# Hybrid decoder layer: the fourth weight sum of the down projection made by accumulating transfers instead of VectorE additions

## The chip, the cores and the metric

The kernel runs on one core of a Trainium2 chip. The metric is the device time of one execution in microseconds, the median of several runs.

## The reference, cut to what matters

One decoder layer in float32: a mixer (short gated convolution beside an mLSTM), a layer norm, a gated MLP with a causal convolution of width 3, and a second layer norm. The change touches only the MLP's last product.

```python
D_MODEL, SEQ, D_FF = 2048, 512, 5632

def conv_ffn(x, w_up, w_ffn_conv, b_ffn_conv, w_down):
    hid = jnp.einsum('bsd,df->bsf', x, w_up)
    hid = causal_dwconv(hid, w_ffn_conv, b_ffn_conv)
    val, gate = hid[..., :D_FF], hid[..., D_FF:]
    return jnp.einsum('bsf,fd->bsd', jax.nn.silu(gate) * val, w_down)

x = layer_norm(alpha * x + mix, ln1_g, ln1_b)
ff = conv_ffn(x, w_up, w_ffn_conv, b_ffn_conv, w_down)
x = layer_norm(alpha * x + ff, ln2_g, ln2_b)
```

## The kernel before

The down projection multiplies the hidden activations (512 tokens by 5632 features) with `w_down` (5632 by 2048). It is a block scheme with seven products in place of eight. The weights are cut into four blocks, A11, A12, A21 and A22, and the products run in the order P1, P2, P6, P5, P7, P3, P4. Products need sums of weight blocks:

- S1: `da21 += w_down[A22]`, an accumulating transfer that GpSimd issues (`down_s1`, L691).
- S2: `dx = da21 + da11`, a VectorE addition (`down_s2`, L1679). P6 reads `dx`.
- S3: `da11 += w_down[A21]`, an accumulating transfer (`down_s3`, L699). P7 reads it.
- S4: `da12 += dx`, a VectorE addition (`down_s4`, L1685). P3 reads it.

The features go through in six chunks of 4, 4, 4, 4, 3 and 3 pairs of 128-row tiles. A slot is one pair of one product: a [128, 1024] weight tile and twelve matmuls of 512 columns. With the products numbered k = 7 * chunk + place, product k of a four-pair chunk has four slots. For each slot ScalarE copies the weight tile to `dslot_hi` in float32r (`down_split`, L1084), VectorE makes the remainder `dslot_lo` (`down_lo_part`, L1655), and TensorE multiplies hi by hi, hi by lo and lo by hi (L1781 to L1783). Both splits run four slots ahead. For each product the hidden block is split likewise (`hid_split` L1101, `hid_lo_part` L1663 and L1666), one product ahead. VectorE adds product k from PSUM to `acc` in the loop of product k + 1 (`add_out`, L1698; ScalarE copies the four first touches, L1127). Product k on TensorE waits until the additions of product k - 2 are done, because PSUM has two sets of banks.

The sums of hidden blocks (T1 to T4, L706, L712, L719, L725) are GpSimd additions of [128, 1024]; in chunk 0 VectorE makes T1 and T2. The residual is added to `acc` by four accumulating transfers of 1 MB (`add_residual`, L732), issued by GpSimd in chunks 0 and 1.

The order of every engine is written out by hand. On GpSimd a chunk is: T1, T2, S3 for pairs 0 and 1, S3 for the rest, T3, T4, then the two S1 of the next chunk, with the residual transfers in between. On SP the loads of the next chunk follow in the order `hb11` (waits for T4), `da21`, `hb12`, `da11`, `hb22`, `da12`, `hb21`, `da22`; the `hb` loads wait for a hidden split and the `da` loads for a slot's `down_lo`. On VectorE the additions S2 and S4 stand after the last slot of a product:

```python
if i in (1, 2, 3) and p == g - 1:
    todo += [("S4", c, a) for a in {1: [0], 2: [1, 2], 3: [3]}[i] if a < g]
if i in (5, 6) and p == g - 1 and c + 1 < CHUNKS:
    todo += [("S2", c + 1, a) for a in {5: [0, 1], 6: [2]}[i]]
```

Accumulating transfers go from GpSimd's queue (q0, software_dynamic), SP's loads from q1 (hardware_dynamic), and both use the same 16 DMA engines.

Of the kernel before, what the change touches and what calls it, by code (L numbers as in the profile page):

```python
# [7 lines left out]
ALU = mybir.AluOpType  # L8
# [26 lines left out]
CHUNK_PAIRS = [4, 4, 4, 4, 3, 3]  # L35
# [95 lines left out]
def build(nc, x_t, x_rows, w_mix, w_out, w_up, w_down, b_gates, conv_w, gain, ln1_cols, ffn_conv,  # L131
          ln1_rows, ln2_rows, ident_in, head_rows_in, causal_in, out):
    ctx = ExitStack()
    with ctx:
# [3 lines left out]
        def sem(name):  # L138
            return ctx.enter_context(nc.semaphore(name))
# [75 lines left out]
        da12 = at("da12", [P, 4, 1024], XB + 16 * KB)  # L215
        da21 = at("da21", [P, 4, 1024], XB)
        da22 = at("da22", [P, 4, 1024], XB + 32 * KB)
        dx = at("dx", [P, 4, 1024], XB + 48 * KB)
# [33 lines left out]
        tile_hi, tile_lo, tile_done = sem("tile_hi"), sem("tile_lo"), sem("tile_done")  # L252
        pads = sem("pads")
        gate_lo, gate_dve, gate_act = sem("gate_lo"), sem("gate_dve"), sem("gate_act")
        gates_ready, gate_turned, gate_cols_ready = sem("gates_ready"), sem("gate_turned"), sem("gate_cols_ready")
        vp_hi, vp_lo, o_sig = sem("vp_hi"), sem("vp_lo"), sem("o_sig")
        qk_h, qk_l = sem("qk_h"), sem("qk_l")
        g_spread, decay_arg, decay_exp, decay_ready = sem("g_spread"), sem("decay_arg"), sem("decay_exp"), sem("decay_ready")
# [31 lines left out]
        acc_in = [sem(f"acc_in{i}") for i in range(4)]  # L290
        s1_added = [sem(f"s1_added{i}") for i in range(2)]
        s3_added = [sem(f"s3_added{i}") for i in range(2)]
        s2_down, s4_down = sem("s2_down"), sem("s4_down")
        t1_sum, t2_sum, t3_sum, t4_sum = sem("t1_sum"), sem("t2_sum"), sem("t3_sum"), sem("t4_sum")
        hc_lo = sem("hc_lo")
        down_hi, down_lo, down_done, half_done = sem("down_hi"), sem("down_lo"), sem("down_done"), sem("half_done")
# [52 lines left out]
        def slot_no(c, i, p):  # L349
            return SLOT0[c] + i * CHUNK_PAIRS[c] + p  # L350
# [10 lines left out]
        def sums_after(s):  # L361

            c, i, p = DOWN[s]
            g = CHUNK_PAIRS[c]
            todo = []
            if i == 0 and c == 0:
                todo.append(("S2", 0, p))
            elif i == 0 and p == 3:
                todo.append(("S2", c, 3))
            if i in (1, 2, 3) and p == g - 1:  # L370
                todo += [("S4", c, a) for a in {1: [0], 2: [1, 2], 3: [3]}[i] if a < g]
            if i in (5, 6) and p == g - 1 and c + 1 < CHUNKS:
                todo += [("S2", c + 1, a) for a in {5: [0, 1], 6: [2]}[i]]
            return todo
# [222 lines left out]
        def _(pool):  # L597
# [96 lines left out]
            def down_s3(c, p):  # L694
# [4 lines left out]
                pool.dma_start(da11[:, p:p + w, :], w_down[A21, :, 1024 * n:1024 * (n + w)].rearrange("p (k n) -> p k n", k=w),  # L699
                               accum_op=ALU.add, max_dma_last_dim=4096).then_inc(s3_added[p // 2], 16)  # L700

            def down_t1(c, g):
                for b in range(2):
                    pool.wait_ge(hb_in[b], 16 * (c + 1))
                pool.wait_ge(hc_lo, NP * c)
                pool.tensor_tensor(hy[:, 0:g, :], hb12[:, 0:g, :], hb11[:, 0:g, :], ALU.subtract).then_inc(t1_sum, 1)  # L706
# [7 lines left out]
            def down_t3(c, g):  # L714
                pool.wait_ge(hb_in[3], 16 * (c + 1))
                pool.wait_ge(t1_sum, OUT_CHUNKS + c + 1)
                if c == 0:
                    pool.wait_ge(down_lo, slot_no(0, 3, 0))
                pool.tensor_tensor(hb12[:, 0:g, :], hb22[:, 0:g, :], hb12[:, 0:g, :], ALU.subtract).then_inc(t3_sum, 1)  # L719
# [16 lines left out]
            for c in range(CHUNKS):  # L736
                g = CHUNK_PAIRS[c]
                if c:
                    down_t1(c, g)
                    down_t2(c, g)  # L740
                for p in range(0, g, 2):
                    down_s3(c, p)
                down_t3(c, g)
                if c == 1:
                    add_residual(0, 1, NP)
                down_t4(c, g)
                if c == 0:
                    add_residual(0, 0, 2)
                if c + 1 < CHUNKS:
                    for p in range(0, CHUNK_PAIRS[c + 1], 2):  # L750
                        down_s1(c + 1, p)
                if c == 0:
                    add_residual(1, 1, 5)
                    add_residual(1, 0, 6)
# [10 lines left out]
        def _(act):  # L765
# [299 lines left out]
            def down_split(s):  # L1065

                c, i, p = DOWN[s]
                what = ORDER[i]
                if s < DOWN_SLOTS:
                    act.wait_ge(up_done, min(N_UP - 2 + s, N_UP))  # L1070
                else:
                    act.wait_ge(down_done, s - DOWN_SLOTS + 1)
                n = sum(CHUNK_PAIRS[:c]) + p
                if what in ("P1", "P2", "P4"):
                    if p == 0:
                        act.wait_ge(da_in[BLOCK[what]], 16 * (c + 1))
                elif what in ("P5", "P7"):
                    if p % 2 == 0:
                        act.wait_ge({"P5": s1_added, "P7": s3_added}[what][p // 2],
                                    16 * (OUT_CHUNKS + sum(CHUNK_PAIRS[a] > p for a in range(c + 1))))  # L1080
                else:
                    act.wait_ge({"P6": s2_down, "P3": s4_down}[what], n + 1)
                src = (da11, da12, da21, da22, dx)[BLOCK[what]]
                act.activation(dslot_hi[s % DOWN_SLOTS][:, :], src[:, p, :], ACT.Copy).then_inc(down_hi, 1)  # L1084

# [59 lines left out]
        def _(dve):  # L1145
# [96 lines left out]
            def mix_work(n):  # L1242
                kind = MIX[n]
                if n - 1 in LAST_QK:
                    h = LAST_QK[n - 1]
                    dve.wait_ge(decay_ready, h + 1)
                    for j in range(NS):
                        dve.wait_ge(scores_done, NS * h + j + 1)
                        s = sc[:, SC_AT[j]:SC_AT[j] + SC_W[j]]
                        dve.scalar_tensor_tensor(s, ps[:, B_S + j % 2, 0:SC_W[j]], Q_SCALE, s, ALU.mult,  # L1250
                                                 ALU.mult).then_inc(p_raw, 1)
                if n == GATES:
                    gates_a()
                if kind[0] == "v" and kind[2] == 3:
                    for c in range(NS):
                        dve.wait_ge(vp_hi, NS * kind[1] + c + 1)
                        dve.tensor_tensor(v_lo[:, c, :, 0:HD], ps[:, B_V + c, :].rearrange("p (h e) -> p h e", h=2),
                                          v_hi[:, c, :, 0:HD].bitcast(F32), ALU.subtract).then_inc(vp_lo, 1)
                if n == GATES + 4:
                    dve.wait_ge(gate_turned, 1)  # L1260
                    dve.tensor_copy(gate_cols[:, :, :, :], ps[:, B_TURN, 0:32].rearrange("p (a c h) -> p a c h", a=2, c=NS)
                                    ).then_inc(gate_cols_ready, 1)
                    dve.wait_ge(gate_cols_ready, 1)
                if kind[0] == "qk":
                    dve.wait_ge(qk_h, 4 * kind[1] + kind[2] + 1)
                    dve.tensor_tensor(qk_lo[:, kind[2], :], ps[:, B_V + kind[2], :],
                                      qk_hi[:, kind[2], :].bitcast(F32), ALU.subtract).then_inc(qk_l, 1)
                h = LAST_QK.get(n)
                if h is not None:
                    dve.wait_ge(g_spread, h + 1)  # L1270
                    if h:
                        dve.wait_ge(p_h, h)
                    for j in range(NS):

                        last = dve.tensor_scalar(sc[:, SC_AT[j]:SC_AT[j] + SC_W[j]], ps[:, B_S, P * j:SEQ],
                                                 gate_cols[:, 0, j, h:h + 1], 0.0, ALU.subtract, ALU.max)
                    last.then_inc(decay_arg, 1)
# [391 lines left out]
            def down_s2(c, p):  # L1669

                if p == 0:
                    dve.wait_ge(da_in[A11], 16 * (c + 1))
                if p % 2 == 0:
                    dve.wait_ge(s1_added[p // 2], 16 * (OUT_CHUNKS + sum(CHUNK_PAIRS[a] > p for a in range(c + 1))))
                if c:
                    dve.wait_ge(s4_down, sum(CHUNK_PAIRS[:c]))
                else:
                    dve.wait_ge(up_done, N_UP - NP + 4)
                dve.tensor_tensor(dx[:, p, :], da21[:, p, :], da11[:, p, :], ALU.add).then_inc(s2_down, 1)  # L1679

            def down_s4(c, p):
                n = sum(CHUNK_PAIRS[:c]) + p
                dve.wait_ge(s2_down, n + 1)
                dve.wait_ge(down_lo, slot_no(c, 1, p) + 1)
                dve.tensor_tensor(da12[:, p, :], da12[:, p, :], dx[:, p, :], ALU.add).then_inc(s4_down, 1)  # L1685

            def add_out(k, u):

# [47 lines left out]
            for s in range(N_DOWN):  # L1736
# [17 lines left out]
                if s == 1:  # L1754
# [1 line left out]
                    dve.wait_ge(t1_sum, OUT_CHUNKS + 1)  # L1756
                    dve.wait_ge(hc_lo, 1)
                    dve.tensor_tensor(hb11[:, 0:g, :], hb22[:, 0:g, :], hy[:, 0:g, :], ALU.subtract).then_inc(t2_sum, 1)
                for what, chunk, pair in sums_after(s):
                    (down_s2 if what == "S2" else down_s4)(chunk, pair)  # L1760
            out_var(0, 12)
            out_var(1, 12)
            finish(0)
# [437 lines left out]
```

## Time and profile before

| what | value |
|---|---|
| median of 3 runs | 2173.48 us (2172.08 to 2177.03) |
| span of the profiled execution | 2176.2 us |
| down projection and last norm in it | from about 1725 us to the end |
| TensorE busy | 2125.9 us, 98% |
| VectorE busy | 1594.2 us, 73% |
| GpSimd busy | 267.1 us, 12% |
| S4 additions on VectorE | 22, 1211 ns each |

The profiled execution has its span alone; it is 2.7 us over the median of the runs and within their spread. Times of the trace are microseconds from the span's start. In a timeline row the two numbers are start and duration, and the bracket at the end is the idle time of the engine ahead of the instruction and what ended it. DMA share is the mean busy share of the 16 DMA engines; over 1.0 means that they were busy without a break.

### The profile page before, as it was taken

What the parts mean: (1) busy time and instruction counts of PE and PEld (TensorE: products, weight loads), DVE (VectorE), ACT (ScalarE), POOL (GpSimd) and SP (SyncE); (2) the same over time, 40 slices, a digit from 0 to 9 for tenths busy, and PEclk for the clock granted to TensorE, in tenths of its full rate; (3) what the DMA queues carried; (4) which work ended last, traced back from release to release, by engine and by line L of the source; (5) the groups of instructions that cost most, each with busy time, mean ns of one, the idle gap of its engine ahead of it and who ended that gap; (6) DMA issues with size and microseconds to landing.
All of it is one profiled execution on the core that took longest, in us unless ns stands there. A gap on an engine that the chain in (4) does not pass through costs nothing. (4 is left out here: it accounts for less than half of the span.)

```text
span 2176.2 us, 26843 instructions
## 1 busy us (share of the span) xinstructions
PE 2125.9 (98%) x10583; PEld 1789.3 (82%) x10583; DVE 1594.2 (73%) x1860; ACT 948.3 (44%) x1107; POOL 267.1 (12%) x241
## 2 busy tenths in 40 slices
PE   9999999999999998999999999999999999999995
PEld 7888888888888887788888888888888788888874
DVE  4354324423338997988888888888888789999998
ACT  3332222221124446555555555555555464444442
POOL 0000000000001304011111111111111023221220
PEclk9999999999999999999999999999999999999998
DMA  6222222242227626888888887887778888775463
GB/s 238 97 97 78 92 89 91 78 171 98 98 79 232 181 73 162 219 241 231 218 207 210 238 219 197 212 229 209 187 203 209 274 228 219 210 237 145 140 193 78
DMA packets 93754, 375.88 MB, mean 173 GB/s; under 512 B 8908, under 2 KB 21228, under 8 KB 80320
## 3 DMA queue, kind: packets, MB, share of 16 engines
q1 hardware_dynamic: 63328, 263.22, 34.4%
q0 software_dynamic: 30304, 110.99, 26.3%
q8 instruction: 82, 1.34, 0.3%
q14 instruction: 40, 0.33, 0.0%
HBM read 326.46 MB, written 26.21 MB: 162 GB/s over the span
## 5 line engine op out<-in xcount | busy, mean ns | idle before, releaser
L1787 PE MATMUL ps<-xb,slot_hi 128*128 128x512 f32 x2408 | 854.5, 400 | 10.2 <-DVE hid L1532 9.8
L1788 PE MATMUL ps<-xb,slot_lo 128*128 128x256 f32 x2400 | 674.4, 281 | 0.0
L1787 PEld LDWEIGHTS ps<-xb,slot_hi 128*128 128x128 f32 x2408 | 453.8, 188 | 126.3 <-issue 12.5
L1788 PEld LDWEIGHTS ps<-xb,slot_lo 128*128 128x128 f32 x2400 | 454.1, 189 | 0.0
L772 ACT ACTIVATE w_hi<-raw 128x2048 fp32r<-128x2048 f32 x56 | 107.3, 1917 | 424.5 <-PE ps L1783 422.0
L1154 DVE TENSOR_TENSOR w_lo<-raw,w_hi 128x2048 fp32r<-128x2048 f32 x55 | 125.8, 2287 | 213.7 <-ACT w_hi L772 213.7
L1781 PE MATMUL ps<-act_hi,w_hi 128*128 128x512 f32 x640 | 249.7, 390 | 0.0
L1783 PE MATMUL ps<-act_hi,w_lo 128*128 128x512 f32 x640 | 249.1, 389 | 0.0
L1782 PE MATMUL ps<-act_lo,w_hi 128*128 128x512 f32 x640 | 249.1, 389 | 0.0
L1501 DVE TENSOR_TENSOR slot_lo<-unit_odd,slot_hi 128x1024 fp32r<-128x1024 f32 x153 | 187.0, 1222 | 36.6 <-ACT slot_hi L974 36.4
L974 ACT ACTIVATE slot_hi<-unit_odd 128x1024 fp32r<-128x1024 f32 x154 | 162.7, 1057 | 106.6 <-PE ps L1788 79.0
L1501 DVE TENSOR_TENSOR slot_lo<-unit_even,slot_hi 128x1024 fp32r<-128x1024 f32 x147 | 179.6, 1222 | 36.0 <-ACT slot_hi L974 35.9
L974 ACT ACTIVATE slot_hi<-unit_even 128x1024 fp32r<-128x1024 f32 x147 | 155.3, 1057 | 93.8 <-PE ps L1788 79.2
L1532 DVE TENSOR_TENSOR hid<-hid,ps 128x256 f32<-128x256 f32 x301 | 126.0, 419 | 42.8 <-ACT hid L1008 32.1
L1781 PE MATMUL ps<-slot_hi,hc 128*128 128x512 f32 x372 | 145.6, 391 | 5.3 <-DVE acc L1698 4.1
L1008 ACT ACTIVATE hid<-ps 128x256 f32<-128x256 f32 x172 | 65.7, 382 | 188.3 <-PE ps L1788 188.3
L1782 PE MATMUL ps<-slot_lo,hc 128*128 128x512 f32 x372 | 144.8, 389 | 0.0
L1783 PE MATMUL ps<-slot_hi,hc 128*128 128x512 f32 x372 | 144.8, 389 | 0.0
L1781 PEld LDWEIGHTS ps<-act_hi,w_hi 128*128 128x128 f32 x640 | 120.1, 188 | 27.0 <-issue 2.3
L1783 PEld LDWEIGHTS ps<-act_hi,w_lo 128*128 128x128 f32 x640 | 120.1, 188 | 24.9
L1782 PEld LDWEIGHTS ps<-act_lo,w_hi 128*128 128x128 f32 x640 | 120.2, 188 | 24.6
L1542 DVE SCALAR_TENSOR_TENSOR yy<-hid,fc,yy 128x511 f32<-128x511 f32 (+1 forms) x172 | 128.4, 747 | 3.9 <-ACT yy L1020 0.9
(238 smaller groups left out, 3431.8 us busy)
## 6 DMA issues: line engine op xcount, KB each, us to landing
raw<-w_mix SPq DMA_DIRECT2D x56, 1024.0 KB, 4.9
unit_odd<-w_up SPq DMA_DIRECT2D x88, 512.0 KB, 6.4
unit_even<-w_up SPq DMA_DIRECT2D x84, 512.0 KB, 6.5
da<-w_down SPq DMA_DIRECT2D x16, 2048.0 KB, 12.6
unit_odd<-w_up POOLq DMA_DIRECT2D x44, 512.0 KB, 8.8
unit_even<-w_up POOLq DMA_DIRECT2D x42, 512.0 KB, 8.4
da<-w_down POOLq DMA_DIRECT2D x20, 1024.0 KB, 9.8
oa<-w_out SPq DMA_DIRECT2D x6, 2048.0 KB, 8.1
```

Source lines behind the costliest of these rows:

```text
L772: act.activation(w_hi[:, s % SPLIT, :], raw[:, s % RAW, :], ACT.Copy).then_inc(tile_hi, 1)
L974: act.activation(slot_hi[(n + 2) % 3][:, :], unit[m % 2][:, BLOCK[ORDER[i]], :], ACT.Copy).then_inc(up_hi, 1)
L1008: act.activation(hid[g % 2][:, t, 256 * half:256 * half + 256], ps[:, up_bank(m, i), 0:256], ACT.Copy).then_inc(hid_act, 1)
L1154: dve.tensor_tensor(w_lo[:, s % SPLIT, :], raw[:, s % RAW, :], w_hi[:, s % SPLIT, :].bitcast(F32), ALU.subtract).then_inc(tile_lo, 1)
L1501: dve.tensor_tensor(lo_slot(n)[:, :], unit[m % 2][:, BLOCK[ORDER[i]], :], slot_hi[(n + 2) % 3][:, :].bitcast(F32), ALU.subtract).then_inc( ...
L1532: dve.tensor_tensor(x, x, cross, ALU.add).then_inc(hid_dve, 1)
L1542: dve.scalar_tensor_tensor(yy[:, t, lag:SEQ], hid[g % 2][:, t, 0:SEQ - lag], fc[:, c + 2 - lag:c + 3 - lag], yy[:, t, lag:SEQ], ALU.mult, ...
L1781: pe.matmul(dst, a[0], b[0], start=first, stop=False, skip_group_check=onto)
L1782: pe.matmul(dst, a[0], b[1], start=False, stop=False, skip_group_check=onto)
L1783: return pe.matmul(dst, a[1], b[0], start=False, stop=last, skip_group_check=onto)
L1787: pe.matmul(dst, a[0], b, start=first, stop=False, skip_group_check=onto)
L1788: return pe.matmul(dst[:, 256:512], a[1], b[:, 0:256], start=False, stop=last, skip_group_check=onto)
```

## The change

The 22 VectorE additions of S4 are taken out. Twelve accumulating transfers take their place, two a chunk, each adding one or two pairs of `dx` to `da12`, from SBUF to SBUF. GpSimd issues them behind T3 and ahead of T4 (in chunk 1 ahead of the residual transfer that stands there too). The semaphore `s4_down` becomes two, one for each half. P3's split on ScalarE and the next chunk's S2 on VectorE wait for the transfer's landing. A semaphore of the gates in the mixer (`gate_cols_ready`) is merged into `gate_dve`, which makes room for the new one.

```diff
-            if i in (1, 2, 3) and p == g - 1:
-                todo += [("S4", c, a) for a in {1: [0], 2: [1, 2], 3: [3]}[i] if a < g]
...
+            def down_s4(c, p):
+
+                n, w = sum(CHUNK_PAIRS[:c]) + p, min(2, CHUNK_PAIRS[c] - p)
+                pool.wait_ge(s2_down, n + w)
+                pool.wait_ge(down_lo, slot_no(c, 1, p) + w)
+                pool.dma_start(da12[:, p:p + w, :], dx[:, p:p + w, :], accum_op=ALU.add, max_dma_last_dim=4096
+                               ).then_inc(s4_down[p // 2], 16)
...
                 down_t3(c, g)
+                for p in range(0, g, 2):
+                    down_s4(c, p)
                 if c == 1:
                     add_residual(0, 1, NP)
                 down_t4(c, g)
...
-                else:
-                    act.wait_ge({"P6": s2_down, "P3": s4_down}[what], n + 1)
+                elif what == "P6":
+                    act.wait_ge(s2_down, n + 1)
+                elif p % 2 == 0:
+                    act.wait_ge(s4_down[p // 2], 16 * sum(CHUNK_PAIRS[a] > p for a in range(c + 1)))
...
-                                    ).then_inc(gate_cols_ready, 1)
-                    dve.wait_ge(gate_cols_ready, 1)
+                                    ).then_inc(gate_dve, 1)
+                    dve.wait_ge(gate_dve, 29)
...
                 if c:
-                    dve.wait_ge(s4_down, sum(CHUNK_PAIRS[:c]))
+                    dve.wait_ge(s4_down[p // 2], 16 * sum(CHUNK_PAIRS[a] > p - p % 2 for a in range(c)))
...
-            def down_s4(c, p):
-                n = sum(CHUNK_PAIRS[:c]) + p
-                dve.wait_ge(s2_down, n + 1)
-                dve.wait_ge(down_lo, slot_no(c, 1, p) + 1)
-                dve.tensor_tensor(da12[:, p, :], da12[:, p, :], dx[:, p, :], ALU.add).then_inc(s4_down, 1)
```

## Rows read from the trace of the kernel before

**Rows 1.** The page: busy time, share of the span and instructions.

```profile
PE 2125.9 (98%) x10583; PEld 1789.3 (82%) x10583; DVE 1594.2 (73%) x1860; ACT 948.3 (44%) x1107; POOL 267.1 (12%) x241
```

**Rows 2.** Windows: stretch, its length, busy time by engine, PEclk, DMA share, GB/s.

```profile
1900.00:1975.00 75.00, 75.00 (x333) 62.10 (x332) 70.65 (x57) 36.40 (x35) 16.91 (x8) 1.00 0.65 193
...
2100.00:2150.00 50.00, 46.96 (x205) 38.35 (x206) 47.54 (x49) 19.82 (x20) 2.75 (x1) 1.00 0.02 5
```

**Rows 3.** Timeline of TensorE: four matmuls that had waited for VectorE.

```profile
1760.59 0.47 PE L1781 MATMUL ps<-slot_hi,hc 128*128 128x512 f32 x1 [0.21 <-DVE acc L1698]
...
1826.58 0.47 PE L1781 MATMUL ps<-slot_hi,hc 128*128 128x512 f32 x1 [0.47 <-DVE acc L1698]
...
2101.34 0.47 PE L1781 MATMUL ps<-slot_hi,hc 128*128 128x512 f32 x1 [1.38 <-DVE acc L1698]
...
2127.87 0.47 PE L1781 MATMUL ps<-slot_hi,hc 128*128 128x512 f32 x1 [1.70 <-DVE acc L1698]
```

**Rows 4.** The tile `dx`: durations min/median/max in ns, first and last start.

```profile
L1679 DVE TENSOR_TENSOR dx<-da,da x22: 1209/1217/3404, 1737.7 to 2092.4; 128x1024 f32<-128x1024 f32 x22
L1685 DVE TENSOR_TENSOR da<-da,dx x22: 1208/1211/1219, 1752.5 to 2121.1; 128x1024 f32<-128x1024 f32 x22
```

**Rows 5.** Timeline of VectorE, last chunk.

```profile
2110.72 0.96 DVE L1663 SCALAR_TENSOR_TENSOR hc<-hy,hc 128x768 fp32r<-128x768 f32 x1 [0.20 <-ACT hc L1101]
...
2119.97 2.35 DVE L1685 TENSOR_TENSOR da<-da,dx 128x1024 f32<-128x1024 f32 x2
...
2126.51 1.21 DVE L1698 TENSOR_TENSOR acc<-acc,ps 128x1024 f32<-128x1024 f32 x1
```

**Rows 6.** Timeline of GpSimd: T3, T4, the S1 transfers, T3 of the last chunk.

```profile
1752.74 5.49 POOL L719 TENSOR_TENSOR hb<-hb,hb 128x1024 f32<-128x1024 f32 x1 [4.38 <-DVE slot_lo L1655]
1758.18 3.39 POOL L725 TENSOR_TENSOR hy<-hb,hb 128x1024 f32<-128x1024 f32 x1
...
1777.99 2.42 POOL L691 DMA_DIRECT2D da<-w_down  x2 [15.27 <-DMA da<-w_down]
...
2094.54 2.17 POOL L719 TENSOR_TENSOR hb<-hb,hb 128x768 f32<-128x768 f32 x1
2111.86 2.75 POOL L725 TENSOR_TENSOR hy<-hb,hb 128x768 f32<-128x768 f32 x1 [15.15 <-DVE hc L1663]
```

**Rows 7.** DMA queues, 1892 to 1904, then 1624 to 1632 us: packets, MB, share.

```profile
q0 software_dynamic: 272, 1.05, 49.7%
...
q0 software_dynamic: 322, 1.12, 72.7%
```

**Rows 8.** Windows by DMA load, columns as in rows 2.

```profile
1760.00:1764.00 4.00, 3.79 (x17) 2.89 (x16) 4.00 (x4) 3.33 (x4) 2.71 (x2) 1.00 0.27 82
1764.00:1828.00 64.00, 63.53 (x281) 52.32 (x280) 55.80 (x43) 34.57 (x35) 16.38 (x10) 1.00 1.03 280
1832.00:1850.00 18.00, 18.00 (x81) 14.92 (x80) 18.00 (x16) 8.63 (x9) 4.82 (x3) 1.00 0.58 188
...
1904.00:1910.00 6.00, 6.00 (x28) 4.99 (x27) 6.00 (x6) 3.23 (x4) 2.85 (x1) 1.00 0.00 0
```

**Rows 9.** DMA queues, 1784 to 1796 us.

```profile
q0 software_dynamic: 374, 1.46, 60.8%
q1 hardware_dynamic: 372, 2.06, 43.8%
```

**Rows 10.** Timeline of VectorE where chunk 0 passes into chunk 1.

```profile
1793.03 2.35 DVE L1679 TENSOR_TENSOR dx<-da,da 128x1024 f32<-128x1024 f32 x2
...
1799.84 1.21 DVE L1698 TENSOR_TENSOR acc<-acc,ps 128x1024 f32<-128x1024 f32 x1
...
1819.07 3.97 DVE L1655 TENSOR_TENSOR slot_lo<-dx,slot_hi 128x1024 fp32r<-128x1024 f32 x1
```

**Rows 11.** Timeline of ScalarE there: two hidden splits.

```profile
1793.56 1.06 ACT L1101 ACTIVATE hc<-hb 128x1024 fp32r<-128x1024 f32 x1 [1.71 <-PE ps L1783]
...
1808.76 1.06 ACT L1101 ACTIVATE hc<-hb 128x1024 fp32r<-128x1024 f32 x1 [6.02 <-DMA hb<-h_dram]
```

More of the change, by code:

```diff
@@ L254, in build @@
         gate_lo, gate_dve, gate_act = sem("gate_lo"), sem("gate_dve"), sem("gate_act")
-        gates_ready, gate_turned, gate_cols_ready = sem("gates_ready"), sem("gate_turned"), sem("gate_cols_ready")
+        gates_ready, gate_turned = sem("gates_ready"), sem("gate_turned")
         vp_hi, vp_lo, o_sig = sem("vp_hi"), sem("vp_lo"), sem("o_sig")
@@ L292, in build @@
         s3_added = [sem(f"s3_added{i}") for i in range(2)]
-        s2_down, s4_down = sem("s2_down"), sem("s4_down")
+        s2_down, s4_down = sem("s2_down"), [sem(f"s4_down{i}") for i in range(2)]
         t1_sum, t2_sum, t3_sum, t4_sum = sem("t1_sum"), sem("t2_sum"), sem("t3_sum"), sem("t4_sum")
@@ L1758, in _ @@
                     dve.tensor_tensor(hb11[:, 0:g, :], hb22[:, 0:g, :], hy[:, 0:g, :], ALU.subtract).then_inc(t2_sum, 1)
-                for what, chunk, pair in sums_after(s):
-                    (down_s2 if what == "S2" else down_s4)(chunk, pair)
+                for _, chunk, pair in sums_after(s):
+                    down_s2(chunk, pair)
             out_var(0, 12)
```

## The prediction

> **What bounds the kernel now.** I read the page first. TensorE is busy for 98% of the span [rows 1]. So an edit counts only where TensorE waits, or where it makes TensorE wait. The windows of the down projection say how much is left to win: in chunks 2 and 3 TensorE has 75.00 busy us in 75.00, its clock granted in full, though VectorE works 70.65 of them [rows 2]. VectorE is nearly full there and still costs nothing. The loss sits at the edges. The timeline of TensorE has waits for the additions to `acc` of 0.21, 0.47, 1.38 and 1.70 us [rows 3] and one more of 0.24, together 4.0. That is all that a relieved VectorE could give in the steady part; the tail behind the last product has no S4 in it.
>
> **What is removed.** 22 additions of 1.21 us [rows 4], which overlap by some 0.08, so about 25 us of VectorE time. Only those are worth anything that stand between VectorE's last idle moment and a wait of TensorE.
> - Last chunk, product P7: VectorE was idle for 0.20 until 2110.72, and from there it runs without a break to the addition at 2126.51, for which TensorE waits 1.70. The pair of S4 at 2119.97 stands in that run [rows 5]. The next instruction starts at 2122.24, so their place is worth 2.27, more than the wait: minus 1.70.
> - Chunk 0, the wait at 1760.59: one S4 at 1752.5 [rows 4] is ahead of it: minus 0.21.
> - The waits at 1826.58 and 2101.34: VectorE has idle moments (at 1812 and 1814, at 2067 and 2075) between the last S4 and them. They stay.
> - The other S4 are hidden under a TensorE that is busy throughout [rows 2]: nothing.
>
> Sum of the removal: minus 1.9 us. If I am wrong on the waits that stay, at most minus 4.0.
>
> **What is added on GpSimd.** Twelve issues, some 1.2 us each by the pair of S1 issues (2.42 for two [rows 6]). Behind them stands T4. In the last chunk GpSimd is idle 15.15 us ahead of T4, and in the chunks from 1 on the idle time there is 8 to 15 us: nothing. In chunk 0 T4 starts straight after T3 [rows 6]; it moves by 2.4 us, from 1758.2 to 1760.6, with the residual transfer and SP's `hb11` load behind it. `hb11` is next needed by T1 at 1802: nothing by itself. A DMA issue does not stretch VectorE's instructions in the trace, while a GpSimd addition does: the remainder at 1819.07 takes 3.97 instead of 1.21 [rows 10]. S4 is a transfer, so nothing is added of that.
>
> **What is added on the DMA engines.** This is the price. No S4 of this size is in the trace; the nearest row is one S3, 1.05 MB accumulated by itself: 49.7% of 12 us, so 6.0 us of all 16 engines [rows 7]. The source there is HBM and for S4 it is SBUF; the half-size sums from SBUF in the up projection ran among others at a similar rate (1.12 MB at 72.7% of 8 us, which is 5.5 us for 1.05 MB [rows 7]). I take 6.0; bounds 5 and 7. A four-pair chunk adds 12 us of DMA work, a three-pair chunk 9.
> - Chunks 2 to 5: S4 follows T3, as at 1896.8, and the engines are idle soon after (share 0.00 from 1904 to 1910 [rows 8]). The transfer lands within some 15 us of T3's end, P3 is split 28 us after it. In the last chunk T3 ends at 2096.7 [rows 6], the window behind has a share of 0.02 [rows 2], and P3's split comes near 2126. Hidden.
> - Chunk 0: T3 ends at 1758.2 [rows 6], the first packets go near 1760. Until 1764 the engines have a share of 0.27, and from 1764 to 1828 it is 1.03, with no idle time in 64 us [rows 8]. Of 12 us some 3 fit ahead; 9 go into a full queue. That is the stretch in which chunk 1 is loaded.
> - Chunk 1: its S4 go out near 1822, with 12 us more; in 1832 to 1850 a share of 0.58 leaves 7.6 us [rows 8], so some 4 us stay when chunk 2 is loaded.
>
> **Who is late.** S1 of chunk 1 was issued at 1777.99 [rows 6], when its load had landed and GpSimd's queue was empty. Now S4 and the residual stand ahead of it in that queue. The two queues take turns: 374 packets against 372 in 12 us, and the software queue's share is 60.8% [rows 9]. The 9 us left shrink by some 2 for the moment in which the queue had stood empty: 7 of work, which is 7 us if the loads lose their place and 11 if they keep half. I take 8. By packet counts the first S1 had landed near 1791 to 1793, and S2 reads it on VectorE at 1793.03 [rows 10] with next to no room. So S2 begins 6 to 8 us late, say 7. Queued behind it on VectorE are the hidden remainder of product 7 and the additions of product 5, which end at 1801.1 [rows 10]; they end at 1808.1. TensorE starts products every 10.88 us; it left one at 1793.3, just ahead of the ScalarE split that it released [rows 11], and wants product 7 at 1804.2. That is a wait of 3.9.
>
> Late next is `hb21`, for which ScalarE waited 6.02 us until 1808.76 [rows 11]. TensorE needs it, split, for product 8 near 1815, or 1819 after the first wait: 3 us are needed for the splits, so the landing may slip by 7. It slips by 7 to 9: 0 to 2, say 0.7. Last, VectorE has 15 us of work from there to the additions of product 7, stretched by T3 (3.97 for one remainder [rows 10]), against 13 that TensorE leaves it: a wait of 2 at product 9 where 0.47 stood, plus 1.5. At the passage to chunk 2, S2 starts at 1869.9 and the later of its two blocks had landed at 1864.0: 6 us of room for the 4 that are left, so nothing.
>
> Sum: minus 1.9, plus 3.9, plus 0.7, plus 1.5, is plus 4.2. On the profile's span 2176.2 gives 2180.4; on the median of the runs, 2.7 lower, it is 2177.7, which I round to 2177.5.
>
> In the Trainium skill ("DMA: Bandwidth & Descriptors", section "Anatomy of one DMA") a transfer on GpSimd's queue is fitted as 2.0 us plus its bytes by 436 GB/s; by that S4 would move in 2.4 us and the two would nearly fit the idle moment, so the time would fall by the 1.9 alone. The trace disagrees: the lone S3 took 6.0 us of the engines. The same page's section "Queues, rings and completion order" says that each engine serves its queues in turns, packet by packet; by that rule, which the equal packet counts here bear out, the loads do not shield S1 from what stands ahead of it.
>
> **The rivals.**
> - *The queue absorbs it* (28 in 100). For it: S1 may have landed earlier than the packet counts say, TensorE has 3 us of room at product 7, and the sum from SBUF may be cheaper. From a delay of S1 of under 4 us TensorE sees nothing. Then minus 1.9 stands alone, with 0 to 1 lost at product 9: 2171.5 to 2173. Against it: a share of 1.03 for 64 us [rows 8]. The page's fit would put the time here.
> - *The backlog runs on into chunk 2* (13 in 100). If the hidden loads of 1 KB packets each wait for a 4 KB accumulate, `hb21` slips by 12 or more, and S4 of chunk 1 does the same to chunk 2. Then 5 more at product 8 and 2 to 4 at chunk 2: 2183 to 2187.
> - *The other side: faster by over 0.2%* (3 in 100). VectorE's relief would have to remove all five waits, 4.0, and GpSimd's T3 in the last chunk would have to meet VectorE more kindly. It decides when TensorE waits no longer at 2101, where two S2 and a remainder stretched by T3 [rows 6] make the lateness without any S4: about 2169.
> - *S4 lands late for P3 of chunk 0.* ScalarE wants its second half at 1777.2 and it lands near 1772 to 1778. A late one eats four slots of lead (10.9 us) first: nothing. It is part of the forecast.
>
> **The numbers.** My forecast, 2173 to 2182, has 56 in 100. The 80% range takes in the absorbed case and the start of the heavy one: 2171.0 to 2184.0. A measurement of this kernel can tell about 0.2%, 4.3 us, so slower begins at 2177.8, in the middle of the forecast. Slower: half of the forecast less a little (27) and all of the heavy case (13), 40. Same: the rest of the forecast (29) and the absorbed case (28), 57. Faster: 3.
>
> **What would show it.** Right: no L1685 on VectorE and its busy time some 25 us lower; L1679 near 1793 idle before it for 5 us or more until a transfer lands; a TensorE wait of 3 to 4 us near 1804 and a longer one near 1829; the software queue busy without a gap from 1760 to about 1850; the wait of 1.70 at P7 of the last chunk gone and the 1.38 ahead of it still there; chunks 2 and 3 unchanged, TensorE full. Wrong: S2 of chunk 1 on time with S4 in the queue (then the sum from SBUF is cheaper than 6 us or the queues don't share as I think), or a ScalarE wait for S4 ahead of P3.

## The result and the profile after

The changed kernel is slower: ratio 1.0047 to the kernel before, 95% interval 1.0031 to 1.0062 (medians of twelve runs each 2187.15 and 2172.78 us). On the 2173.5 of the prediction the ratio gives 2183.7, 0.3 us inside its range; the median itself lies above it. The sign is that of the forecast. The size is 10 us by the ratio (14 by the medians), where 4 were forecast.

The page of the profile after, busy time as in [rows 1]:

```profile
PE 2128.0 (97%) x10583; PEld 1791.9 (82%) x10583; DVE 1572.7 (72%) x1838; ACT 949.7 (43%) x1107; POOL 277.3 (13%) x253
```

VectorE is 21.5 us less busy, with 22 instructions fewer. The span is 9.3 us longer. In this execution the down projection also began 1.3 us earlier than in that of before, so times of the two traces are compared with that in mind. The waits of TensorE in the down projection, timeline rows that answer to [rows 3]:

```profile
1824.58 0.76 PE L1785 MATMUL ps<-slot_hi,hc 128*128 128x512 f32 x1 [10.67 <-ACT acc L1137]
...
1825.57 0.63 PE L1787 MATMUL ps<-slot_hi,hc 128*128 128x512 f32 x1
...
2112.58 0.47 PE L1785 MATMUL ps<-slot_hi,hc 128*128 128x512 f32 x1 [1.38 <-DVE acc L1702]
```

One wait of 10.67 us is new: it is the start of product 8, P2 of chunk 1. The 0.21, the 0.47 and the 1.70 of before are gone; the 1.38 has stayed, and so have two small ones, 0.24 ahead of it and one at 2042 in the trace before (0.31) and at 2053 after (0.46). The windows say two more things (columns as in [rows 2]):

```profile
1764.00:1824.00 60.00, 49.91 (x220) 40.84 (x218) 38.25 (x30) 24.07 (x25) 11.60 (x7) 0.96 1.05 287
...
1824.00:1828.00 4.00, 3.42 (x8) 2.78 (x9) 3.37 (x4) 4.00 (x5) 0.00 (x0) 0.50 0.37 138
...
1900.00:1975.00 75.00, 75.00 (x333) 62.10 (x332) 66.37 (x53) 36.38 (x35) 19.28 (x10) 1.00 0.81 224
```

The loss sits in 1764 to 1824, where the DMA engines have no idle moment (share 1.05). Chunks 2 and 3 run with TensorE full, as before. And behind its wait TensorE gets half its clock (0.50, the level of 1.2 GHz): its matmuls start 0.43 us apart instead of 0.23 until 1829.4, some 11 of them at about 0.2 more each, which costs 2.3 us.

The chain that ended last, in the same stretch, names what TensorE waited for (start, duration, what):

```profile
1783.60 35.96 DMA hb<-h_dram
...
1820.62 1.04 ACT slot_hi L1094
1821.66 0.91 ACT acc L1137
...
1823.42 1.02 ACT acc L1137
...
1824.58 0.76 PE ps L1785
```

The load of `hb21` took 36.0 us from its issue; it was 23.6 before. ScalarE stood at the hidden split that reads it, the second row here answering to [rows 11]; ahead of it is the last slot split before the wait:

```profile
1800.24 1.07 ACT L1094 ACTIVATE slot_hi<-da 128x1024 fp32r<-128x1024 f32 x1 [1.65 <-PE ps L1787]
1819.66 1.06 ACT L1111 ACTIVATE hc<-hb 128x1024 fp32r<-128x1024 f32 x1 [18.36 <-DMA hb<-h_dram]
```

Behind that split in ScalarE's order stand a slot split, a first-touch copy of product 6, another slot split and the second copy. TensorE's product 8 waits for both copies, because they empty the PSUM banks that it writes. So its wait is put down to a ScalarE copy, while the cause is a transfer four instructions ahead of it.

GpSimd, in answer to [rows 6]:

```profile
1756.05 2.42 POOL L705 DMA_DIRECT2D da<-dx  x2
1757.56 3.36 POOL L731 TENSOR_TENSOR hy<-hb,hb 128x1024 f32<-128x1024 f32 x1
1759.90 2.18 POOL L738 DMA_DIRECT2D acc<-res_dram  x1
...
1782.29 2.42 POOL L689 DMA_DIRECT2D da<-w_down  x2 [20.21 <-DMA da<-w_down]
```

And the DMA queues, in windows of 1764 to 1776, 1776 to 1784 and 1808 to 1816 us (columns as in [rows 7]):

```profile
q0 software_dynamic: 511, 1.99, 89.9%
q1 hardware_dynamic: 474, 0.53, 15.3%
...
q1 hardware_dynamic: 774, 3.40, 103.5%
q0 software_dynamic: 9, 0.00, 0.3%
...
q0 software_dynamic: 378, 1.42, 88.9%
q1 hardware_dynamic: 379, 0.39, 17.4%
```

The first pair shows the mechanism. S4 and the residual transfer keep GpSimd's queue full while SP's queue holds `hb11`, in 512 packets of 1 KB. While both have work, the two queues move nearly equal numbers of packets, so that 0.53 MB of loads move beside 1.99 MB of sums; before, the same 12 us moved 2.52 MB of loads beside 1.04 MB. The second pair shows GpSimd's queue empty: S1 can only be issued when `da21` has landed, at 1782.3 instead of 1778.0, and it found nothing ahead of it. The third pair is `hb21` itself: 379 packets of 1 KB against 378 that are nearly all of 4 KB.

VectorE at the passage, in answer to [rows 10]:

```profile
1794.60 2.36 DVE L1689 TENSOR_TENSOR dx<-da,da 128x1024 f32<-128x1024 f32 x2 [2.92 <-DMA da<-w_down]
...
1801.42 1.21 DVE L1702 TENSOR_TENSOR acc<-acc,ps 128x1024 f32<-128x1024 f32 x1
```

S2 waited 2.92 us for S1. By the clock it began only 1.6 us later than before; against TensorE, which ran 1.4 us earlier here, it was 3.0 late. TensorE did not feel it.

### The profile page after: what moved, and what is told of

It is laid out like the page before. It is cut to its first block and busy times, and to the rows that moved or that the text cites. A ratio compares the mean times of both kernels' runs of the same rounds, so it can differ in the third digit from the quotient of the medians.

```text
span 2185.5 us, 26813 instructions
## 1 busy us (share of the span) xinstructions
PE 2128.0 (97%) x10583; PEld 1791.9 (82%) x10583; DVE 1572.7 (72%) x1838; ACT 949.7 (43%) x1107; POOL 277.3 (13%) x253
## 5 line engine op out<-in xcount | busy, mean ns | idle before, releaser
L1511 DVE TENSOR_TENSOR slot_lo<-unit_even,slot_hi 128x1024 fp32r<-128x1024 f32 x147 | 179.7, 1223 | 35.6 <-ACT slot_hi L982 35.4
L1785 PE MATMUL ps<-slot_hi,hc 128*128 128x512 f32 x372 | 146.5, 394 | 13.7 <-ACT acc L1137 10.7
## 6 DMA issues: line engine op xcount, KB each, us to landing
da<-w_down SPq DMA_DIRECT2D x16, 2048.0 KB, 12.9
```

Source lines behind the costliest of these rows:

```text
L1511: dve.tensor_tensor(lo_slot(n)[:, :], unit[m % 2][:, BLOCK[ORDER[i]], :], slot_hi[(n + 2) % 3][:, :].bitcast(F32), ALU.subtract).then_inc( ...
L1785: pe.matmul(dst, a[0], b[0], start=first, stop=False, skip_group_check=onto)
```

## The experiments

Runs of one kernel spread over up to 19 us here, and in several kernels they lie in two groups about 8 us apart (the twelve of e11: six from 2163.7 to 2168.0, six from 2173.1 to 2176.6). The profiles place this spread mostly ahead of the down projection, which began between 1715 and 1728 us. So beside each ratio stands the length of the down projection in the profiled run, from the first to the last start of a matmul that reads `hc`. It was 427.4 us before and 437.9 after. Each kernel has one profiled execution; the ratios rest on twelve runs of each kernel, nine of e2 and four of e9.

| kernel | ratio | 95% interval | down projection, us | wait at product 8, us |
|---|---|---|---|---|
| before | 1 | | 427.4 | 0 |
| after | 1.0047 | 1.0031 to 1.0062 | 437.9 | 10.67 |
| e1 chunk 0 on VectorE | 0.9985 | 0.9969 to 1.0002 | 432.9 | 2.88 |
| e2 only chunk 0 by transfer | 1.0050 | 1.0032 to 1.0069 | 440.8 | 10.47 |
| e10 before, with traffic added | 1.0062 | 1.0041 to 1.0084 | 438.4 | 10.44 |
| e3 after, residual late | 0.9978 | 0.9961 to 0.9994 | 425.4 | 0 |
| e11 the same again | 0.9975 | 0.9957 to 0.9993 | 426.5 | 0 |
| e4 after, 4 KB pieces | 0.9996 | 0.9981 to 1.0012 | 423.5 | 0 |
| e5 before, 4 KB pieces | 1.0001 | 0.9982 to 1.0021 | 426.0 | 0 |
| e6 before, residual late | 0.9996 | 0.9976 to 1.0016 | 425.9 | 0 |
| e12 the same again | 0.9997 | 0.9981 to 1.0014 | 426.8 | 0 |
| e8 after, both cures | 1.0006 | 0.9991 to 1.0021 | 422.7 | 0 |
| e13 the same again | 0.9993 | 0.9979 to 1.0007 | 423.9 | 0 |
| e9 after, ScalarE reordered | 1.0049 | 1.0030 to 1.0068 | 437.6 | 9.27 |

**Which chunk.** Chunk 0's S4 back on VectorE, all others by transfer; the waits for S4 are changed to match:

```diff
+S4_DMA = (1, 2, 3, 4, 5)
...
+            if c not in S4_DMA and i in (1, 2, 3) and p == g - 1:
+                todo += [("S4", c, a) for a in {1: [0], 2: [1, 2], 3: [3]}[i] if a < g]
...
-                for p in range(0, g, 2):
-                    down_s4(c, p)
+                if c in S4_DMA:
+                    for p in range(0, g, 2):
+                        down_s4(c, p)
```

> Chunk 0's four S4 sums are VectorE additions again, chunks 1 to 5 keep the accumulating transfers. Theory A (the loss comes from chunk 0's two transfers alone: 12 us of DMA work in a full stretch make the hidden load hb21 of chunk 1 land 11 us late, and ScalarE, which waits for it, holds back TensorE): TensorE's wait of 10.7 us near 1824 is gone, the wait of 1.70 at P7 of the last chunk stays gone, and the time is 1 to 2 us under the kernel before, ratio 0.9990 to 1.0000. Theory B (the loss is spread over the chunks, by the later landing of each S4 or by GpSimd's order): at least half of the loss stays, ratio 1.002 or more.

The second has `S4_DMA = (0,)`, the reverse.

> The reverse: only chunk 0's S4 are transfers, chunks 1 to 5 keep the VectorE additions. Theory A: the whole loss is here, one TensorE wait of 10 to 12 us at product 8, and the 1.70 at P7 of the last chunk is back, so a little slower than the changed kernel: ratio 1.005 to 1.0065. Theory B: a sixth to a third of the loss, ratio under 1.002.

Measured 0.9985, a little under what was expected, and 1.0050. The loss belongs to chunk 0's two transfers; the ten others cost nothing that can be measured. The merged semaphore of the gates costs nothing measurable either, since e1 has it as well. e2 has a wait of 1.71 at P7 of the last chunk back, e1 does not. One thing was not expected in e1: its profile has a wait of 2.88 at product 8, where the kernel before had none:

```profile
1816.96 0.77 PE L1800 MATMUL ps<-slot_hi,hc 128*128 128x512 f32 x1 [2.88 <-ACT acc L1143]
```

The work of chunk 0 and its order are the same in both, but `hb21` took 28.1 us in this execution and 23.6 in that of before. The load had next to no room already (1.5 us, see below), and these two executions differ by three times that. Behind this wait too the granted clock was 0.50, in the windows from 1817 to 1823. Its 432.9 us hold 2.88 of wait, some 3 lost at the lower clock, and 2.3 more wait at the projection's start than before (2.85 against 0.59). That wait differs between executions of equal code as well, 0.95 in e3 and 2.16 in e11. In e2 it was 2.48, and the clock was 0.50 behind it until 1738; with the 1.71 at P7 this gives e2 the longest down projection.

**Is it traffic alone.** The kernel before, its S4 all on VectorE, with two accumulating transfers of 1 MB whose sums nothing reads. They start from `dx` like S4 but end in DRAM; only the next overwrite of `dx` waits for them:

```diff
                 down_t3(c, g)
+                if c == 0:
+                    pool.wait_ge(res_z_in, 16 * PIECES)
+                    for p in (0, 2):
+                        pool.wait_ge(s2_down, p + 2)
+                        pool.dma_start(zn_dram[p // 2].rearrange("p (k n) -> p k n", k=2), dx[:, p:p + 2, :],
+                                       accum_op=ALU.add, max_dma_last_dim=4096).then_inc(t_in, 16)
...
                 if c:
+                    dve.wait_ge(t_in, 48)
```

> The kernel before, its S4 sums all on VectorE, with two transfers of 1 MB added where chunk 0's S4 would be issued: they accumulate dx onto a DRAM buffer that is no longer read, nothing in the computation waits for them but the next overwrite of dx. Theory A (DMA traffic alone makes the loss): the same single wait of about 10 us at product 8, ratio 1.004 to 1.006. Theory C (S4's own landing or its removal from VectorE matters): ratio 0.999 to 1.001.

Measured 1.0062, just over the 1.006 that was expected. The same single wait is there, without any S4 transfer and without a change on VectorE:

```profile
1823.34 0.77 PE L1788 MATMUL ps<-slot_hi,hc 128*128 128x512 f32 x1 [10.44 <-ACT acc L1133]
```

Its `hb21` took 35.6 us, and S2 waited 2.52 us for S1, not for the added transfers. So neither the landing of S4 nor the thinned-out VectorE is needed for the loss; the traffic alone makes it.

**Relieving the queue.** The changed kernel with the four residual transfers moved by two chunks:

```diff
+RES = 2
...
-                pool.wait_ge(added, 2 * adds)
+                pool.wait_ge(added, 2 * (NP * RES + adds))
...
-                if c == 0:
+                if c == RES:
                     add_residual(0, 0, 2)
...
-                if k >= NP:
+                if k >= NP * (RES + 1):
                     dve.wait_ge(acc_in[2 * th + fd], 16)
```

> The changed kernel, but the four residual transfers (1 MB each, accumulating, from GpSimd's queue) are issued in chunks 2 and 3 instead of 0 and 1. Theory A (a backlog of DMA work in general): the stretch from 1760 to 1830 loses 3 of its residual transfers, 18 us of DMA work, more than the 12 that S4 added; hb21 lands at 1809 or earlier, TensorE's wait at product 8 is gone: ratio 0.998 to 1.000. Theory C (it is S4's dependences: the landing of S4 itself, the order of issues on GpSimd): nothing changes, ratio 1.005.

> The changed kernel with the residual transfers in chunks 2 and 3, a second time (0.9978 before). Theory A: the down projection is 2 us shorter than in the kernel before, so 0.998 to 1.000; the first result was on the low side of that by the spread of the runs.

Measured 0.9978 and 0.9975, both just under the range that was expected, while the down projection of the second was 0.9 us shorter than before and not 2. `hb21` took 18.8 us in the first. ScalarE no longer waits for it, and both first-touch copies are done by 1808.3:

```profile
1803.53 1.06 ACT L1112 ACTIVATE hc<-hb 128x1024 fp32r<-128x1024 f32 x1 [1.71 <-PE ps L1788]
...
1807.30 1.01 ACT L1138 ACTIVATE acc<-ps 128x1024 f32<-128x1024 f32 x1
```

The same move in the kernel before:

> The kernel before with the four residual transfers in chunks 2 and 3. The control for the changed kernel with them there (0.9978). Theory A: the crowd at chunk 0 thins out and costs TensorE 0.5 us at most in the kernel before, so 0.9990 to 1.000; the S4 transfers with an empty queue are worth the 1.9 us of VectorE on top, which a ratio of two kernels hardly shows. Rival: the later residual transfers themselves are worth the 0.2%, whatever S4 is.

> The kernel before with the residual transfers in chunks 2 and 3, a second time (0.9996 before), beside the changed kernel with them there. Theory A: down projection 1.5 us shorter than before, ratio 0.999 to 1.000, between the kernel before and the changed one so placed.

Measured 0.9996 and 0.9997, with a down projection 1.5 and 0.6 us shorter than before (1.5 was expected of the second too). So the move alone is worth nothing that can be told from no change, while with S4 by transfer the kernel came out faster than before twice, by 0.2%. The difference to e6 and e12 is within the intervals. The profiles show what belongs to it, the missing 1.70 of the last chunk and the missing 0.2 of chunk 0, but longer waits at the start and at two small places take part of it back: the down projection is only 0.5 us (e3 against e6) and 0.3 (e11 against e12) shorter. The medians of e3 and e11 fall between the two groups of runs, six and six, and those of e6 and e12 into the upper group. Compared group by group, e3 is 0.9 and 1.8 us below e6, and e11 0.7 and 4.0 below e12. So a gain of the forecast 1.9 us fits, once the traffic has room; that it is 0.2% is not shown.

**Packets or bytes.** The changed kernel with the hidden activations laid out so that a load reads 4 KB in one piece:

```diff
-        h_dram = nc.dram_tensor("h_dram", (NF, P, SEQ), F32).ap()
+        h_dram = nc.dram_tensor("h_dram", (P, 2, NF, 256), F32).ap()
...
-                sp.dma_start(h_dram[t], prod[t % 2][:, :]).then_inc(h_out[t % 2], 16)
+                sp.dma_start(h_dram[:, :, t, :], prod[t % 2][:, :].rearrange("p (h t) -> p h t", h=2)).then_inc(h_out[t % 2], 16)
...
-                             h_dram[t:t + pairs, :, 256 * (b % 2):256 * (b % 2) + 256].rearrange("k p t -> p k t")
+                             h_dram[:, b % 2, t:t + pairs, :]
```

> The changed kernel with the hidden activations kept in DRAM as [128, 2, 44, 256] in place of [44, 128, 512]: a load of a hidden block reads 4 KB in one piece per partition (128 pieces) instead of four of 1 KB (512 pieces); the bytes are the same, the stores go out in pieces of 1 KB instead of 2 KB. Theory A1 (hb21 is late because each 1 KB packet waits for one 4 KB packet of the other queue): with a quarter of the packets a hidden load takes 3 to 4 us in the full stretch instead of 12, hb21 lands 15 us or more earlier, the wait at product 8 is gone: ratio 0.998 to 1.000. Theory A2 (bytes count, not packets): hb21 is as late as before, ratio 1.004 to 1.006.

Measured 0.9996, and the wait at product 8 is gone with all of S4's traffic in place. `hb21` took 23.1 us instead of 36.0 (12.9 less, where 15 or more were expected), and ScalarE waited 5.51 for it. Its queues in 1808 to 1816 us:

```profile
q1 hardware_dynamic: 128, 1.82, 54.6%
q0 software_dynamic: 191, 0.77, 48.3%
```

SP's queue moves 1.82 MB there, where the changed kernel moved 0.39. The load is as many bytes in a quarter of the packets, so it was late by its number of packets and not by its bytes. A wait of 0.96 for an addition has appeared at product 7, the place at which I had forecast 3.9. VectorE's S2 waited for S1 there for longer than in the changed kernel:

```profile
1797.80 2.36 DVE L1689 TENSOR_TENSOR dx<-da,da 128x1024 f32<-128x1024 f32 x2 [4.02 <-DMA da<-w_down]
```

A wait of 2.92 cost TensorE nothing and one of 4.02 cost it 0.96: on this path there are 3 us of room.

> The kernel before with the hidden activations in DRAM as [128, 2, 44, 256], so that a hidden load is 128 pieces of 4 KB. It is the control for the changed kernel with the same layout (0.9996). Theory A: without S4 transfers the hidden load hb21 was on time by 1.5 us already, so nothing large is to be had: ratio 0.999 to 1.000. If the layout alone is worth 10 us wherever it stands, it would be 0.995.

Measured 1.0001: the layout alone is worth nothing measurable where `hb21` was on time.

**Both cures.**

> The changed kernel with both cures: residual transfers in chunks 2 and 3 and hidden blocks in pieces of 4 KB. Theory A: the crowd is gone by either cure alone, so both together give no more than the better one: ratio 0.997 to 0.999, TensorE's only waits left in the down projection are the start's and 1.4 at P2 of the last chunk.

> The changed kernel with both cures, a second time (1.0006 before, with a shorter down projection in the profile). Theory A: 0.997 to 0.999. If it is 1.000 or more again while the down projection is shorter again, the up projection is longer by the stores in pieces of 1 KB, and the layout is not a gain.

Measured 1.0006 and 0.9993, against 0.997 to 0.999 expected: outside in both, though the second's interval reaches into it. The down projection is among the shortest, 422.7 and 423.9 us (423.5 in e4), though it began late in the first, at 1727.0. What is shorter is mostly TensorE's waits at the start of the projection. Whether the stores in pieces of 1 KB lengthen the up projection stays open: the down projection began at 1728.2, 1722.0, 1727.0 and 1722.8 with them, 1725.0 in the mean, and between 1715.1 and 1724.9 without, 1720.8 in the mean of ten. That points to a longer up projection, but the spread is as large as the difference.

**ScalarE's order.** In the first product of a chunk the hidden split goes behind the two copies:

```diff
+                late = c and i == 0
-                if p == 0:
+                if p == 0 and not late:
...
+                if p == 1 and late:
+                    hid_split(c, 1)
+                    down_split(s + DOWN_AHEAD - 1)
+                    down_split(s + DOWN_AHEAD)
```

> The changed kernel with one reordering on ScalarE: in the first product of chunks 1 to 5 the hidden split that waits for hb21 stands behind the two first-touch copies to acc instead of ahead of them. hb21 lands as late as before. Theory A (ScalarE's order puts the two copies, two slot splits and the hidden split, 4.9 us, between the landing and TensorE's start): now only the splits stand there, about 3.2 us, so the wait at product 8 falls from 10.7 to about 9, ratio 1.003 to 1.006. If the landing alone counted, 10.7 stays.

Its wait is 9.27 us, now for VectorE's remainder and no longer for the copy; ratio 1.0049. The order is worth 1.4 us of the 10.7 by this profile, the transfer the rest.

## Why the prediction was right in its sign and too small

- **What VectorE's relief is worth.** Right. The 1.70 at P7 of the last chunk and the 0.21 of chunk 0 are gone, the 1.38 stayed, chunks 2 and 3 are unchanged. The waits that I had listed as 4.0 lacked the 0.31 at 2042.04; it stayed too. VectorE's busy time fell by 21.5 us and not 25: S4 was 26.2 in the down projection, but the remainders of the weight tiles took 2.7 more there (180.9 against 178.2), and the rest I did not trace.
- **What is added on GpSimd.** T4 of chunk 0 was to move by 2.4 us. It started at 1757.56, by the clock 0.6 earlier than before, because T3 took 4.35 us instead of 5.49 and T4 started before the second issue was over.
- **The size of one transfer.** Forecast 6.0 us of the engines per 1 MB. In 1908 to 1922, with SP's queue nearly idle, GpSimd's queue moved 738 packets at 104.6%, which is 5.4 us for the 272 packets of one transfer. The end of an S3 is among them; 1912 to 1920, in the midst of the two S4, gives 5.4 as well (425 packets at 106.2%). Slightly cheaper, within the bounds.
- **Where it hurts.** Right: chunk 0's S4 run into the full stretch (e1, e2, e10), and chunk 1's do not matter.
- **"S1 stands behind S4 in the queue"** is the step that failed. GpSimd's queue had run empty at 1776, because SP's loads had been held up and S1 depends on one of them, `da21`. S2 was 3.0 us late against TensorE (1.6 by the clock), not 7. That is within the 3 us of room, and the 3.9 at product 7 did not come.
- **"Late next is `hb21`, 0 to 2"** is the term that was mis-sized, 0.7 forecast and 10.67 measured, and both halves of it were off. The slip: ScalarE's split went from 1808.76 to 1819.66, 10.9 us by the clock and 12.3 against TensorE, which ran 1.4 us earlier; the transfer itself took 12.4 longer. I had 7 to 9. The room: I had 7, of which 3.9 was the wait at product 7 that did not come. In the rest I had counted 3 us from the landing to TensorE's start, for the two splits; it was 4.9 to the end of the second first-touch copy, which stands behind the hidden split on ScalarE and which product 8 waits for. In the kernel before, that copy ended at 1813.5 and product 8 began at 1815.2: room of 1.5 to 1.7. A slip of 12.3 less that room is the wait of 10.67. The slip of 12 or more stands in the prediction as the heavy rival, with 13 in 100: hidden loads whose 1 KB packets each wait for a 4 KB one. That half of the rival came true; its other half, a loss of 2 to 4 at chunk 2, did not, since TensorE has no wait there.
- **"A wait of 2 at product 9"**, plus 1.5, did not come. Instead the 0.47 at that place went. In e10, with all of S4 on VectorE and the same long stop of TensorE just before that place, it went as well. It is also missing in e5 and e6, without a stop, where `hb21` took only 16.4 and 14.0 us. So it seems to hang on that load and on TensorE's pace, not on S4; no run separates the two.
- **The clock.** Not in the prediction. A TensorE that stood for 10.7 us restarted at half its clock, 2.3 us more.

So of the four terms minus 1.9, plus 3.9, plus 0.7 and plus 1.5, the first was right, the second and the fourth did not come, and the third was 10 us too small. That the ratio still falls inside the range is luck.

The sum by what was measured: 10.7 for the wait and 2.3 for the clock, less 1.7, 0.5 and 0.2, plus 0.3 at the start of the projection (0.86 against 0.59) and 0.15 at 2053 (0.46 against 0.31), is 11.0. The down projection is 437.9 - 427.4 = 10.5 us longer; 0.5 I did not trace.

The Trainium skill ("DMA: Bandwidth & Descriptors", section "Queues, rings and completion order") says that each DMA engine takes the queues with work in turns, packet by packet. The rows agree: 379 packets against 378. What I had not drawn from it is its consequence: at equal turns the queue with the smaller packets gets the smaller share, here 0.39 MB against 1.42. By the fit in the Trainium skill's section "Anatomy of one DMA" of the same page, the movement of 1 MB is estimated at 2.4 us; the trace has 5.4 for these accumulating transfers.

What stays open: why the load of `hb21` takes 23.6 us in one execution and 28.1 in another with the same work up to there, and the two groups of run times.

## What to carry to other kernels

Moving work from a busy engine to transfers cost nothing here where the DMA engines had time left (a share of 0.81 in 1900 to 1975, with the new transfers in it) and 10 us where they had none. The price appeared at another queue. So follow the transfers that share the window to their consumer, and count everything that stands between that consumer's wait and TensorE in its engine's order. With queues that take turns by packet, the load in packets of 1 KB beside accumulating ones of 4 KB was the one to fail; larger pieces, or moving other traffic out of the window, gave the loss back. A busy share of 1.03 over 64 us is a full stretch: before adding to it, take something out.

## What the runs showed of the hardware that was not expected

- Two queues with work moved equal numbers of packets, 379 to 378 in 8 us, though those of one are 1 KB and nearly all of the other 4 KB, so a 0.5 MB load in 1 KB pieces took 36.0 us from issue to landing, and 23.1 in 4 KB pieces.
- After 10.7 us without a matmul TensorE ran at a granted clock of 0.50 for some 5 us (one matmul every 0.43 us instead of 0.23). After a wait of 2.88 us in e1 it did so for 6 us, some 3 lost, although a wait of 2.85 in the same execution, at 1735, left the clock at 1.00. In e2 a wait of 2.48 at that same place was followed by 0.50 until 1738, 1.7 lost. So a short wait can cost about twice its length, or only its length.
- An accumulating transfer of 1 MB from SBUF to SBUF took the engines 5.4 us, a little less than the one from HBM that the prediction goes by (6.0).
